# A hybrid decoder step on one core: page numbers read ahead of the buffer wait, and two spare buffers handed over one gate item earlier

## The reference

```python
ik_past = cache_ik[page_table].reshape(DB, past, IDX_DIM)
idx, valid = indexer_select(iq, iw, ik_all, q_pos, jnp.arange(L), topk)
phys = take_rows(page_table, p_pos // ps)
k_sel = jnp.where(is_new, take_rows(k_new, n_pos), cache_k[phys, off])
v_sel = jnp.where(is_new, take_rows(v_new, n_pos), cache_v[phys, off])
s = jnp.einsum('bqhd,bqkhd->bqhk', q, k_sel) * (DSA_HEAD_DIM ** -0.5)
p = jax.nn.softmax(jnp.where(valid[:, :, None, :], s, -jnp.inf), axis=-1)
o = jnp.einsum('bqhk,bqkhd->bqhd', p, v_sel)
return (o.reshape(B, L, DSA_WIDTH) * jax.nn.silu(g)) @ w_out
```

## Time and profile before

| | before |
|---|---|
| median of 3 runs | 1209.37 us (1208.86 to 1212.71) |
| the profiled execution | 1208.89 us |
| its span, first to last instruction | 1207.1 us |
| mean granted clock of TensorE | 0.996 |
| busy: PE, DVE, ACT, POOL | 96%, 50%, 46%, 32% |
| DMA queue of SP | 152.59 MB, 38.8% of 16 engines |

### The profile page before, as it was taken

One profiled execution on the slowest core, in us unless ns is written; L12 is line 12 of the kernel. 1 busy time (PEld: TensorE's weight loads), 2 busy tenths in 40 slices (PEclk: granted clock), 3 DMA queues, 4 the chain that ended last, 5 costly groups with the idle time before them and its releaser, 6 DMA issues. The chain is left out here.

```text
span 1207.1 us, 25033 instructions
## 1 busy us (share of the span) xinstructions
PE 1162.4 (96%) x9937; PEld 1026.0 (85%) x9937; DVE 601.3 (50%) x1183; ACT 557.9 (46%) x1088; POOL 381.8 (32%) x322
## 2 busy tenths in 40 slices
PE   8999999999999999999999989999999999999897
PEld 6889887898678998888965549999999889988797
DVE  6462355756079999010015544589266253245652
ACT  6542466544324355444544444432454344266643
POOL 5544131245313511122200013534445254411330
PEclk9999999999999999999999999999999999999999
DMA  5235235133505256767669882232321136234212
GB/s 183 76 113 162 75 115 183 45 84 93 182 1 178 71 182 213 237 232 218 221 236 409 334 312 87 72 104 71 124 77 38 36 105 192 71 105 158 88 36 74
DMA packets 127788, 168.78 MB, mean 140 GB/s; under 512 B 20384, under 2 KB 93480, under 8 KB 127663
## 3 DMA queue, kind: packets, MB, share of 16 engines
q1 hardware_dynamic: 115609, 152.59, 38.8%
q10 hardware_dynamic: 12062, 14.59, 3.4%
HBM read 150.70 MB, written 16.81 MB: 139 GB/s over the span
## 5 line engine op out<-in xcount | busy, mean ns | idle before, releaser
L671 POOL TENSOR_TENSOR w_lo<-raw,w_hi 128x512 fp32r<-128x512 f32 (+2 forms) x267 | 359.9, 1379 | 729.5 <-ACT w_hi L1425 729.5
L707 PE MATMUL psum<-h_hi,w_hi 128*128 128x272 f32 x1616 | 471.6, 292 | 6.0 <-DVE h_lo L2343 4.7
L709 PE MATMUL psum<-h_hi,w_lo 128*128 128x272 f32 x1616 | 467.2, 289 | 0.0
L708 PE MATMUL psum<-h_lo,w_hi 128*128 128x272 f32 x1616 | 464.8, 288 | 0.0
L707 PEld LDWEIGHTS psum<-h_hi,w_hi 128*128 128x128 f32 x1616 | 303.4, 188 | 16.8 <-issue 12.3
L708 PEld LDWEIGHTS psum<-h_lo,w_hi 128*128 128x128 f32 x1616 | 303.7, 188 | 0.1
L709 PEld LDWEIGHTS psum<-h_hi,w_lo 128*128 128x128 f32 x1616 | 302.9, 187 | 0.0
L1425 ACT ACTIVATE w_hi<-raw 128x1024 fp32r<-128x1024 f32 (+1 forms) x137 | 135.5, 1035 | 114.5 <-PE psum L709 79.5
L707 PE MATMUL psum<-w_hi,h_hi 128*128 128x512 f32 (+2 forms) x352 | 124.6, 354 | 0.0
L709 PE MATMUL psum<-w_hi,h_lo 128*128 128x512 f32 (+2 forms) x352 | 121.0, 344 | 0.0
L708 PE MATMUL psum<-w_lo,h_hi 128*128 128x512 f32 (+2 forms) x352 | 120.9, 343 | 0.0
(11 more groups left out here) (327 smaller groups left out, 1493.6 us busy)
## 6 DMA issues: line engine op xcount, KB each, us to landing
raw<-in_cache_k_dram SPq DMA_DIRECT2D x128, 256.0 KB, 3.1
raw<-in_gla_w_in_dram SPq DMA_DIRECT2D x23, 1024.0 KB, 5.4
spare<-in_cache_v_dram SPq DMA_DIRECT2D x36, 512.0 KB, 6.4
raw<-in_dsa_w_in_dram SPq DMA_DIRECT2D x17, 1024.0 KB, 6.4
raw<-in_cache_v_dram SPq DMA_DIRECT2D x28, 512.0 KB, 6.0
gla_s_in<-in_state_gla_dram SPq DMA_DIRECT2D x16, 512.0 KB, 7.9
raw<-in_gla_w_out_dram SPq DMA_DIRECT2D x8, 1024.0 KB, 6.9
out_dram<-gla_s_in ACTq DMA_DIRECT2D x16, 512.0 KB, 4.1
```

The source lines that it names most:

```text
L671: pool.tensor_tensor(copies(key, pair_view(w_lo, key)[:, k]), raw_copies(key, k), copies(key, pair_view(w_hi, key)[:, k].bitcast(F32)), AL ...
L707: pe.matmul(out, lh, rh, start=start, stop=False)
L708: pe.matmul(out, lh, rl, start=False, stop=False)
L709: return pe.matmul(out, ll, rh, start=False, stop=stop)
```

## The change

First, SP reads the page numbers of a key or value unit (four or two) into registers ahead of the wait for its slot, where before it read each one just ahead of its DMA. Second, the two spares of the first output item's pair (4 and 6) are marked as held by gate item 2, the other two by gate item 3, where before all four were held by gate item 3. Third, whatever is held by gate item 2 counts as free only from key unit 29 on, so raw slot 1 is not chosen for the key units before that either.

```diff
             if held_by[s] is None:
                 return -1, s
+            if held_by[s] == (dsa_at, "g", 2):
+                return index[(dsa_at, "K", 29)] - 0.5, s
             return index[first] - 0.5 if s >= RAW and items[index[held_by[s]]][4] == "w" else index[held_by[s]], s
...
                 if key == values[0]:
-                    held_by.update({s: (dsa_at, "g", 3) for s in range(RAW, RAW + SPARE)})
+                    for x in range(2):
+                        held_by.update({s: (dsa_at, "g", 2 + (x != first_out)) for s in spares_of(x)})
...
                 L = key[0]
 
+                page_at = []
+                for x in range(kk if kind != "w" else 0):
+                    grp, pg, part = key[2] // (2 * NPAGE), key[2] // 2 % NPAGE, key[2] % 2
+                    col = (4 * grp + (x if kind == "K" else 2 * part + x)) * NPAGE + pg
+                    page_at.append(sp.value_load(ptab[0:1, col:col + 1], min_val=0, max_val=cache_k.shape[1] - 1))
                 s, old = slot[key], before[key]
...
-                    for x in range(kk):
-                        grp, pg, part = key[2] // (2 * NPAGE), key[2] // 2 % NPAGE, key[2] % 2
-                        col = (4 * grp + (x if kind == "K" else 2 * part + x)) * NPAGE + pg
-                        r = sp.value_load(ptab[0:1, col:col + 1], min_val=0, max_val=cache_k.shape[1] - 1)
+                    for x, r in enumerate(page_at):
+                        part = key[2] % 2
```

## The result

| | before | changed |
|---|---|---|
| median | 1209.37 us (1205.55 to 1213.83, 13 runs) | 1212.43 us (1209.81 to 1215.17, 13 runs) |
| the profiled execution | 1208.89 us | 1210.36 us |
| its span | 1207.1 us | 1208.5 us |

The ratio is 1.0031 (95% interval 1.0021 to 1.0041): slower by 3 to 4 us. The forecast was no change, 1208.9 us; the time lies in the range, near its upper end, and the sign of the small change was missed. Lines of the changed kernel stand 6 further down (L1228 is L1234, L1334 is L1340, L1317 is L1323, L1425 is L1431), and the address and DMA line L539 is L545.

The account below looks back on a forecast made before the run. TensorE, busy 96% of 1207.1 us, bounds the kernel, so only its idle time or low clock counts. -6.7 + 4.7 + 1.2 - 4.1 + 6.2 + 0.8 - 2.6 = -0.5 us gives 1208.9 us, range 1204.6 to 1213.4.

Parts of the forecast that it names:

- part 1: Key units: page numbers loaded ahead of the slot wait remove all of PE's six waits there; -6.7 us.
- part 2: Key units 26 and 27 wait some 1.2 and 3.5 us, sharing two slots with gate item 3; +4.7 us.
- the spares: Value phase: earlier value loads remove the 2.49 us wait at the second page and its slow page; -4.1 us.
- Part 3: First output item: ACT's split moves to prompt unit 24, waits for the item and delays PE's copy; +6.2 us.
- Part 4: Last value page: PE comes 6 us later, so the 1.00 us wait and the slow page vanish; -2.6 us.
- a sign against this part: Key units: if key waits stay before unit 26, the claim that the early page numbers remove them is wrong.
- +1.2: Low clock behind the waits at key units 26 and 27: between 0 and 1.65 us, taken as +1.2 us.
- Rival A: Output item's split: ACT's wait does not reach PE, and the last page's gain is not won; 1204.5 us, chance 0.12.
- some 8 us: Sign: ACT's split of the output item comes some 8 us after PE's page 12 started.
- +0.8: Low clock behind PE's wait for ACT at the first output item: 0 to 1.65 us, taken as +0.8 us.
- the landing at 5.1 us: Key units: four pieces land 5.1 us after their slot's release, 2.05 us less than before.
- Rival B: Wherever a unit is waited for, close pieces crowd the DMA engines, long waits return at low clock; 1213.1 us, chance 0.13.

Follow-up runs that it names:

- experiment 1: Kernel before plus only the page numbers read ahead of the wait; slots, spares and output item's split as before: 1200.97 us, ratio 0.9951 to the kernel before.
- experiment 3: Changed kernel with the first output item's split back at prompt unit 28, nothing else: 1210.47 us, ratio 1.0010 to the kernel before.
- experiment 8: Changed kernel once more, unedited, to see how its time goes with its clock: 1212.11 us, ratio 1.0022 to the kernel before.
- experiment 5: Changed kernel with raw slot 1 kept for key units, output item behind the last value unit and split at prompt unit 29: 1197.05 us, ratio 0.9905 to kernel before.
- experiment 6: Changed kernel with the first output item's split at prompt unit 22 instead of 24: 1219.16 us, ratio 1.0087 to the kernel before.

## Why the prediction was off

PE's timeline cut at four places gives each part its measured size, forecast and profiled execution alike:

| stretch | forecast | measured | from |
|---|---|---|---|
| to key unit 25 (part 1 but for 595.21) | -5.9 | -5.89 | 570.69 - 576.58 |
| key unit 25 to 28 (part 2, less the 0.78 of 595.21) | +5.1 | +6.02 | 24.65 - 18.63 |
| key unit 28 to page 12 (the spares) | -4.1 | -4.22 | -4.09 - 0.13 |
| page 12 to the end of page 15 (parts 3 and 4) | +4.4 | +5.40 | 1.31 + 4.09 |
| sum | -0.5 | +1.3 | span +1.4 |

*Part 1.* Right in kind, a little too large, and the match in the table is luck. The wait at 541.06 stayed, 0.93 us, which the prediction itself had named as a sign against this part. The release came at 534.9 and the last piece landed at 541.0: 6.1 us, not 5.1. Two other waits that went had 5.7 to 5.9 us from release to landing and PE just came after. In return 0.55 us of the 5.89 was there by key unit 0 (420.71 against 421.26), ahead of any wait of this change, so the part gave some 5.3 us. In experiment 1, which has this edit alone, the way from key unit 0 to unit 28 is 5.9 us shorter (168.1 against 173.9 us), where the prediction has 6.7.

*Part 2, the shared slots.* The place and the kind of both waits were right, with 2.04 and 3.08 us where 1.2 and 3.5 stood: 5.12 against 4.7. The term "+1.2" for the clock was too small. 6.02 - 5.12 + 0.78 leaves 1.68 us: transposes of 3.02 instead of 1.97 us, and the weight matmuls behind them. The landing was too short here too. SP issued the four pieces of unit 26 from 572.8 to 574.4, 0.53 us apart as forecast, but they landed in up to 4.3 us, not in 3.0:

```profile
L545 SPq DMA_DIRECT2D raw<-in_cache_k_dram x4: 332/332/333, 572.8 to 574.4; - x4
...
DMA to landing us min/median/max: 2.7/3.7/4.3
```

I had taken the landing from pieces issued 1.1 us apart.

*The spares.* Right: no wait and no slow page at 627.93. But experiment 1 showed that the first edit alone would have taken most of it (a wait of 0.75 us instead of 2.49, and no low clock), which the prediction does not say; the sum is not touched by that, only whose gain it is.

*Part 3.* The mechanism came as described, step by step: ACT's wait for the item, the split of 2.0 us, and a wait of PE of 6.04 us before L1323 where 6.2 stood. Rival A is out by this row. The item was issued at 696.0, landed 6.9 us later, at 702.9, which is 10.0 us after page 12 started; the "some 8 us" among the prediction's signs doesn't fit its own sum (706.9 - 697.05 = 9.9). The term "+0.8" for the clock was the one that failed: the low level lasted 6.9 us here, page 14 alone paid 3.64 - 1.92 = 1.72 us.

*Part 4.* Right: no wait, no slow page at 715.05. That ACT's delay is what hides this wait in the changed kernel is borne out by experiment 3, where the delay is gone and the last page waits 2.24 us; against the kernel before, the first edit alone removes it too (experiment 1).

So in the profiled execution the mechanism held and the failed step is the size of **the clock behind the waits**: the terms +1.2 and +0.8. It was 1.68 us in the key units and, since 5.40 - 6.04 + 1.00 + 1.65 leaves 2.0, about that behind ACT's wait: 3.7 us where 2.0 stood, nearly all of the 1.8 us by which the table misses. The prediction took both ends from a single row, one slow page (0 to 1.65 us), and chose inside them; the truth was at or above the upper end. That row, 712.09 of before, follows a wait of 1.00 us and not the one of 2.49 us beside which the prediction puts it (the page from 630.36 on took about as long, to 633.9). A wait of 1.00 us was followed by the low level and one of 1.75 us was not, so its own rows already showed that the length of the wait alone does not set this price.

The forecast has a gain and a loss of some 13 us each that nearly cancel, so an error of under 2 us was enough to turn -0.5 into +1.3.

The rest, from the +1.3 us of this execution to the +3.1 us of the medians, is how executions differ. Over 46 runs of the kernel before the time fell by 0.89 us for each 0.001 of mean granted clock (correlation -0.85), over 25 of the changed kernel by 0.88 us (-0.80), and the mean clock was 0.9950 in the one and 0.9924 in the other. If all of that slope were the clock's doing, 2.6 x 0.89 = 2.3 of the 3.45 us between the means would be clock, where the forecast has -1.3 (1.2 + 0.8 - 1.65 - 1.65). That is an upper bound: the second profile of the changed kernel (experiment 8) shows that its slower execution had longer waits too, for key units above all, and there the second failed term stands, **the landing at 5.1 us**, which was 5.7 to 6.1 us wherever it was read. No kernel here holds the clock while it keeps the waits, so the two are told apart in the two profiles only. Experiments 1 and 5, which take the long waits away, have a clock of 1.00 over the key and value phases. How much of the last 1.8 us is clock and how much is waits stays open.

Rival B named 1213.1 us, nearer to the result than the forecast, and was half right. Its clock part (both long waits come back fully at the low level) held. Its crowding came only in part: 0.93 us of key waits stayed where it has 0.6, but the item landed in 6.9 us, as in the forecast (700.1 to 706.9), and unit 27 in 5.7 us after its release (582.11 to 587.80) instead of 5.1; the pieces were issued 0.53 us apart and came in with 0.6 us of delay, not 1.1. The rule of the Trainium skill that stood beside it ("TensorE: Matmul & The Clock Gate", "What's actually happening": the low clock is the default and activity lifts it) was the better guide than the value chosen from one row. By it the sum was +0.8, and the trace agrees (+1.3). It agrees only so far: in experiment 3 the low level stayed for 10 us while PE was busy for all of them. The other page of the Trainium skill that the prediction names ("DMA: Bandwidth & Descriptors", "Where 436 GB/s comes from", about 358 GB/s from HBM) is not borne out here. The item landed when 408 GB/s had it, and the changed kernel has 394 GB/s in 627:632; the measurement decides.

```profile
627.00:632.00 5.00, 4.67 (x29) 1.67 (x25) 2.46 (x11) 3.93 (x8) 0.00 (x0) 1.00 0.99 394
```

What stays open: why nearly the same wait is followed by 3.4 us of low clock in one execution and 6.8 us in another (3.08 and 3.24 us at key unit 27), and what delayed the pieces at 535 to 541 us.

## What to carry to other kernels

An operation that can be done ahead of a wait is cheap to move, and here it won some 6 us by itself; judge it apart from the reshuffling that comes with it. When a plan of buffers changes, follow every number that is derived from it: here "the last unit in this pair" moved ACT's split by four steps onto a load that had not arrived. Where PE is 96% busy, price a wait with what the clock does behind it too, from several waits and several executions; its length alone does not give that price.

## What the runs showed of the hardware that I had not expected

- The low clock at a wait lasted from 3.4 us to 17 us, and it went on while PE was fully busy (10.00 of 10.00 us in 713:723 of experiment 3, at 0.50). Its length did not follow the wait's: a wait of 1.00 us (before, last page) was followed by 3.4 us, 2.24 us by 10 us, and 3.08 us by 3.4 us. The longest, in experiment 6, began inside the wait of 10.57 us, which ended at 707.69, so about half of the 17 us cost nothing:

```profile
697.00:708.00 11.00, 0.43 (x3) 0.31 (x2) 0.00 (x0) 3.00 (x6) 1.87 (x2) 0.60 0.57 191
708.00:716.00 8.00, 6.39 (x28) 2.92 (x28) 3.54 (x13) 1.65 (x7) 3.52 (x3) 0.50 0.00 1
```

- Single waits of up to 1.75 us among key units were followed by no low clock in any profile (before: 1.00 behind 1.75 us; experiment 1: 1.00 over 540:600 with one of 0.9 us), nor was the one of 2.04 us at unit 26 of the changed kernel (1.00 over 578:584).
- Pieces of 256 KB issued 0.53 us apart landed in 2.7 to 4.3 us, against 2.5 to 3.1 us at 1.10 us apart.
